# Latent attention of a two-layer block: keys and queries in tiles of 128 columns, rotary rows exchanged by Vector's shuffle, two query tiles moved behind the first score items

## The reference

```python
qa, ka, va, cq, ckv, kr, gates = jnp.split(h @ w_in, IN_SPLITS, axis=-1)
q  = heads(_rmsnorm(cq, g_q) @ w_uq, 8)      # 768 -> 8 heads x (64 plain + 32 rotary)
kv = heads(_rmsnorm(ckv, g_kv) @ w_ukv, 8)   # 256 -> 8 heads x (64 key + 64 value)
q_mla = _mla_q(qn, _axial_rope(qr, ang_r, ang_c))            # per head: 64 plain, 32 turned
k_mla = concat([k_ctx_mla, _mla_k(kn, _axial_rope(kr, ...))])  # one turned 32-row key for all heads
o_mla = softmax(q_mla @ k_mla.T * 96**-0.5) @ v_mla          # 8 heads, 512 x 768 scores
```

## Time and profile before

| what | value |
|---|---|
| median of 3 runs | 2316.14 us (2315.51 to 2317.17) |
| span of the profiled execution, first to last instruction | 2309.8 us |
| rotary key, latents and their norm, PE | 1612.8 to 1677.5 us |
| keys and values, PE | 1677.6 to 1705.1 us |
| queries, PE | 1705.1 to 1744.1 us |
| attention items 0 to 31 | 1744.1 to 1834.3 us |
| PE busy over the span | 2248.2 us (97%) |

### The profile page before, as it was taken

The page is one execution under the profiler, slowest core; times in us unless marked ns, Lnnn a source line. Parts: engine busy times, 40 slices in busy tenths (PEclk is TensorE's granted clock), DMA queues, the critical chain, the costliest instruction groups (busy, mean ns, idle before and its releaser), DMA issues.

```text
span 2309.8 us, 35228 instructions
## 1 busy us (share of the span) xinstructions
PE 2248.2 (97%) x12694; PEld 1935.9 (84%) x12694; DVE 1309.3 (57%) x2094; ACT 966.7 (42%) x1500; POOL 1300.6 (56%) x1448
## 2 busy tenths in 40 slices
PE   7999999999999999999999999999999999999997
PEld 6768787678888889999999979877866887999997
DVE  3424632498878778464454563243137556876666
ACT  4454544544233454332332343355435535444443
POOL 3434465099978766564654533322446064977775
PEclk9999999999999999999999999999999999999999
DMA  4222232255655542221222212222230031323232
GB/s 162 87 82 74 73 119 93 110 175 198 198 192 193 192 135 74 73 73 58 79 65 72 75 55 91 79 80 76 78 96 28 1 110 65 99 94 110 92 110 74
DMA packets 68241, 230.54 MB, mean 100 GB/s; under 512 B 7296, under 2 KB 12672, under 8 KB 67968
## 3 DMA queue, kind: packets, MB, share of 16 engines
q1 hardware_dynamic: 51232, 177.92, 23.3%
q10 hardware_dynamic: 16864, 50.60, 6.6%
HBM read 225.61 MB, written 2.10 MB: 99 GB/s over the span
## 4 chain that ended last, share of the span: by engine, by line
PE 82%; DVE 8%; issue 4%; ACT 3%; POOL 2%; DMA 0%; DVEq 0%; POOLq 0%; ACTq 0%; SPq 0%
PE ps L2304 20%; PE ps L2810 11%; PE ps L2308 10%; PE ps L2869 7%; PE ps L2866 6%; PE ps L2865 6%; PE ps L3013 4%; PE ps L2360 3%; POOL WLO L443 1%; PE ps L2315 1%; PE ps L2955 1%; PE ps L2984 1%; PE ps L2998 1%; PE ps L3152 1%; PE ps L3135 1%
## 5 line engine op out<-in xcount | busy, mean ns | idle before, releaser
L443 POOL TENSOR_TENSOR WLO<-RAW,WHI 128x256 fp32r<-128x256 f32 x1004 | 868.7, 900 | 739.3 <-ACT WHI L542 738.7
L542 ACT ACTIVATE WHI<-RAW 128x1024 fp32r<-128x1024 f32 x251 | 263.2, 1057 | 290.5 <-DMA RAW<-in_stream_dram 287.1
L462 POOL TENSOR_TENSOR WLO<-RAW,WHI 128x256 fp32r<-128x256 f32 x240 | 235.6, 1002 | 197.3 <-DVE SRAW L1913 82.4
L2304 PE MATMUL ps<-HLO,WHI 128*128 128x512 f32 (+2 forms) x872 | 317.4, 380 | 0.0
L2304 PE MATMUL ps<-HHI,WHI 128*128 128x512 f32 (+2 forms) x872 | 309.9, 371 | 0.0
L2308 PE MATMUL ps<-HHI,WLO 128*128 128x512 f32 (+2 forms) x872 | 198.4, 371 | 0.3 <-POOL WLO L443 0.3
L2304 PEld LDWEIGHTS ps<-HLO,WHI 128*128 128x128 f32 (+1 forms) x872 | 159.4, 188 | 33.5 <-issue 4.0
L2304 PEld LDWEIGHTS ps<-HHI,WHI 128*128 128x128 f32 (+1 forms) x872 | 159.3, 188 | 31.9 <-issue 3.4
L2308 PEld LDWEIGHTS ps<-HHI,WLO 128*128 128x128 f32 (+1 forms) x872 | 153.8, 188 | 29.2 <-POOL WLO L443 0.5
L2810 PE MATMUL ps<-GLO,WHI 128*128 128x384 f32 (+1 forms) x480 | 143.7, 353 | 1.3 <-POOL WLO L443 1.2
L2810 PE MATMUL ps<-GHI,WHI 128*128 128x384 f32 (+1 forms) x480 | 143.5, 353 | 0.0
(11 more groups left out here) (507 smaller groups left out, 5364.3 us busy)
## 6 DMA issues: line engine op xcount, KB each, us to landing
RAW<-in_stream_dram SPq DMA_DIRECT2D x331, 512.0 KB, 3.3
ADA<-in_ada_dram ACTq DMA_DIRECT2D x72, 512.0 KB, 4.4
BM<-in_bias_dram ACTq DMA_DIRECT2D x8, 448.0 KB, 3.7
DECAY<-in_decay_dram ACTq DMA_DIRECT2D x4, 512.0 KB, 4.2
C<-in_ctx_dram ACTq DMA_DIRECT2D x2, 1024.0 KB, 5.5
out_dram<-X SPq DMA_DIRECT2D x16, 128.0 KB, 1.8
X<-in_x_dram SPq DMA_DIRECT2D x2, 512.0 KB, 5.7
X<-in_x_dram ACTq DMA_DIRECT2D x2, 512.0 KB, 6.6
```

Of the source, the lines that this page charges most:

```text
L443: op = nc.gpsimd.tensor_tensor(WLO[:, slot(u), k:k + 2], RAW[:, slot(u), k:k + 2], WHI[:, slot(u), k:k + 2].bitcast(F32), ALU.subtract)
L462: op = nc.gpsimd.tensor_tensor(WLO[:, j, k:k + 2], RAW[:, j, k:k + 2], WHI[:, j, k:k + 2].bitcast(F32), ALU.subtract)
L542: nc.scalar.activation(WHI[:, j], RAW[:, j], ACT.Copy).then_inc(unit_hi, 1)
L2304: nc.tensor.matmul(out, high[k], x[:, k, tok], start=(k == 0 and n == 0), stop=False)
```

## The change

The weight columns of `w_ukv` and `w_uq` are laid out anew. The first `ukv` unit now holds the keys of all heads, two heads to a tile of 128 columns; the second holds all values. The `uq` units are six instead of eight: two tiles with the rotary rows of four heads each (32 rows a head, no padding), four tiles with the plain rows of two heads each. The permutation matrices are gone: DVE exchanges the rotary rows with `stream_shuffle` (i to i^8 in each group of 32 partitions). On PE the order becomes keys 0, keys 1, values 0 and 1, keys 2, values 2 and 3, keys 3, values 4 and 5, then four query tiles, score items 0 and 1, the last two query tiles, score item 2. ACT issues the eight key-spreading DMAs in one row after the keys, copies the last query tiles between exponentials of items 1 and 2, and rounds the weight units `o`+1 and `o`+2 inside the attention (after items 10 and 12) instead of beside the queries. `MP`, `MPT` and `KHI` change places. The constants shrink from seven 128x128 matrices to five.

```diff
-("ukv", 2), ("uq", 8), ("o", 8),
+("ukv", 2), ("uq", 6), ("o", 8),
+ROTATED = [i ^ 8 for i in range(32)]
-UKV_BANKS = (3, 2, 0, 1, 0, 1, 2, 3)
-UQ_BANKS = (3, 0, 1, 2)
+UKV_BANKS = (3, 2, 0, 1)
+MV_BANKS = (6, 7, 4, 5, 0, 1)
...
+        def roped_at(h):
+            return s("mq_rope"), 7 * (h // 4) + 3 + h % 4 + 1
...
-                sp.dma_start(const[:], t["const"][:, 0:7 * P]...
+                sp.dma_start(const[:], t["const"][:, 0:CONSTS * P]...
...
# POOL: lows(UNIT["na_q"], UNIT["o"] + 1) before the heads are split; split_head now waits
             pool.wait_ge(*attend_at("s", 3))
             pool.wait_ge(s("kr_spread"), 128)
+            pool.wait_ge(*roped_at(7))
...
# ACT, attend
+                    if n == 1:
+                        query_copy(2)
+                        query_copy(3)
+                    if n in (10, 12):
+                        convert(UNIT["o"] + n // 2 - 4)
...
# ACT, after the norm of cq
-            for h in range(8):
-                act.wait_ge(s("mk_ready"), h + 1)
-                nc.scalar.activation(MK[0:64, h], psf[0:64, at:at + N2], ACT.Copy).then_inc(s("mk"), 1)
+            for q in range(4):
+                if q < 3:
+                    act.wait_ge(s("mk_ready"), q + 1)
+                else:
+                    wait_unit(UNIT["ukv"])
+                for p in range(2):
+                    nc.scalar.activation(MK[0:64, 2 * q + p], psf[64 * p:64 * p + 64, at:at + N2], ACT.Copy).then_inc(s("mk"), 1)
+                if q == 1:
+                    convert(UNIT["ukv"] + AHEAD)
+                    act.dma_start(COSQ...); act.dma_start(SINQ...)
             convert(UNIT["ukv"] + AHEAD + 1)
-            act.wait_ge(s("kr_rope"), 3)
-            for h in range(8):
-                convert(UNIT["uq"] + AHEAD + h)
-                wait_unit(UNIT["uq"] + h)
-                nc.scalar.activation(q[0:QK_MLA, h % 4], ps[0:QK_MLA, UQ_BANKS[h % 4]], ACT.Copy).then_inc(s("mq_raw"), 1)
-                if h < 4:
-                    for i in (2 * h, 2 * h + 1):
-                        act.dma_start(MK[64:QK_MLA, i], KR2[64:QK_MLA]).then_inc(s("kr_spread"), 16)
+            act.wait_ge(s("kr_rope"), 4)
+            for i in range(8):
+                act.dma_start(MK[64:QK_MLA, i], KR2[64:QK_MLA]).then_inc(s("kr_spread"), 16)
+            convert(UNIT["uq"] + 3)
+            convert(UNIT["uq"] + 4)
+            def query_copy(a):
+                wait_unit(UNIT["uq"] + 2 + a)
+                bank = (4, 5, 7, 6)[a]
+                for p in range(2):
+                    nc.scalar.activation(query(2 * a + p)[0:64], ps[64 * p:64 * p + 64, bank], ACT.Copy).then_inc(s("mq_raw"), 1)
+            convert(UNIT["uq"] + 5)
+            query_copy(0)
+            convert(UNIT["o"])
+            query_copy(1)
...
# DVE
-                    if n == 1:
-                        query_rope(7)
+            def query_rope(i):
+                x, turned, n = ps[:, 6 + i], RQ[:, i], 7 * i
+                wait_unit(UNIT["uq"] + i)
+                V.stream_shuffle(turned, x, ROTATED)
+                V.tensor_tensor(x, x, COSQ[:], ALU.mult)
+                V.tensor_tensor(turned, turned, SINQ[:], ALU.mult)
+                for j in range(4):
+                    r = slice(32 * j, 32 * j + 32)
+                    V.tensor_tensor(query(4 * i + j)[64:QK_MLA], x[r], turned[r], ALU.add)
+            query_rope(0)
+            query_rope(1)
...
# PE, attend
+                    if n == 1:
+                        pe.wait_ge(*roped_at(7))
+                        query_tile(4, 7)
+                        query_tile(5, 6)
...
+                        if k == 0:
+                            pe.wait_ge(s("mq_raw"), 4)
# PE, before it
-            nc.tensor.matmul(ps[0:QK_MLA, 6], const[0:QK_MLA, SWAPM, 0:QK_MLA], KR2[0:QK_MLA, 0:S], ...)
+            def latent_keys(q):
+                pe.wait_ge(*norm_at("cq", *(("rs", 1), ("lo", 2), ("lo", 4), ("lo", 6))[q]))
+                mm = unit(UNIT["ukv"], 0, [(ps[:, 2 * j], x_tok), (ps[:, 2 * j + 1, 0:M], ctx_tok)], kt=2, k0=2 * q, ...)
+            def latent_values(b):
+                pe.wait_ge(s("mk"), 2 + 2 * (b // 2))
+                ... 6 matmuls of 512 columns into ps[:, MV_BANKS[b]]
+            latent_keys(0)
+            latent_keys(1)
+            wait_weights(UNIT["ukv"] + 1)
+            latent_values(0)
+            latent_values(1)
+            latent_keys(2)
+            latent_values(2)
+            latent_values(3)
+            latent_keys(3)
+            latent_values(4)
+            latent_values(5)
+            def query_tile(i, bank):
+                unit(UNIT["uq"] + i, 0, [(ps[:, bank], x_tok)], kt=6, hi=CQHI, lo=CQLO)
+            for i in range(4):
+                pe.wait_ge(s("mv"), i + 1)
+                query_tile(i, (6, 7, 4, 5)[i])
...
-                if n == 1:
-                    turn_query(7)
```

More of the change, by code:

```diff
@@ L267, in build, with query @@
         (MQBL,), _ = region(c_at, ("MQBL", [P, 4, S], F32R))
+        def query(h):
+            return MQA[:, h] if h < 4 else MQB[:, h - 4]
         def query_low(h):
@@ L3107, in turn_query @@
-            def turn_query(h):
-                pe.wait_ge(s("mq_raw"), h + 1)
-                if h >= 4:
-                    pe.wait_ge(s("mq_rope"), 3 * (h - 4) + 3)
-                nc.tensor.matmul(ps[0:QK_MLA, 4 + h % 4], const[0:QK_MLA, SWAPM, 0:QK_MLA], (MQA if h < 4 else MQB)[0:QK_MLA, h % 4],
-                                 start=True, stop=True).then_inc(s("mq_swap"), 1)
-            for h in range(8):
-                pe.wait_ge(*((s("mk"), 6), (s("mv"), 4), (s("mv"), 5), (s("mv"), 6))[h] if h < 4 else (s("mq_raw"), h - 3))
-                unit(UNIT["uq"] + h, 0, [(ps[0:QK_MLA, UQ_BANKS[h % 4]], x_tok)], kt=6, hi=CQHI, lo=CQLO, cols=(0, QK_MLA))
-                if h == 1:
-                    pe.wait_ge(s("mk"), 8)
-                if h:
-                    turn_query(h - 1)
+            def latent_keys(q):
+                pe.wait_ge(*norm_at("cq", *(("rs", 1), ("lo", 2), ("lo", 4), ("lo", 6))[q]))
+                j = UKV_BANKS[q]
+                mm = unit(UNIT["ukv"], 0, [(ps[:, 2 * j], x_tok), (ps[:, 2 * j + 1, 0:M], ctx_tok)], kt=2, hi=CVHI, lo=CVLO,
+                          k0=2 * q, last=(q == 3))
+                if q < 3:
+                    mm.then_inc(s("mk_ready"), 1)
@@ new lines, in latent_values @@
+            def latent_values(b):
+                pe.wait_ge(s("mk"), 2 + 2 * (b // 2))
+                j = slot(UNIT["ukv"] + 1)
+                for k in range(2):
+                    wh, wl = WHI[:, j, k:8:2, :], WLO[:, j, k:8:2, :]
+                    for n, (x, w) in enumerate(((CVHI, wh), (CVLO, wh), (CVHI, wl))):
+                        mm = nc.tensor.matmul(ps[:, MV_BANKS[b]], x[:, k, b * P:(b + 1) * P], w, start=(k == 0 and n == 0),
+                                              stop=(k == 1 and n == 2))
+                mm.then_inc(*((s("mv_ready"), 1) if b < 5 else (units_done, 1)))
@@ L3326, in layout @@
     w = g["w_ukv_2"][0]
-    for n in range(8):
-        units(UNIT["ukv"] + n // 4, w, P * n, n=1, k0=2 * (n % 4))
-    units(UNIT["uq"], g["w_uq_2"][0], cols=QK_MLA)
+    for part in range(2):
+        heads = w.reshape(2 * P, 8, 2, 64)[:, :, part].reshape(2 * P, 512)
+        for n in range(4):
+            units(UNIT["ukv"] + part, heads, P * n, n=1, k0=2 * n)
+    w = g["w_uq_2"][0].reshape(6 * P, 8, QK_MLA)
+    units(UNIT["uq"], w[:, :, 64:].reshape(6 * P, 256))
+    units(UNIT["uq"] + 2, w[:, :, :64].reshape(6 * P, 512))
     units(UNIT["o"], g["w_o_na_2"][0])
```

131 lines of the change are left out of this document (55 added, 76 removed).

## The result

The changed kernel takes **2289.46 us** in the median (2288.79 to 2290.53), beside 2316.65 for the kernel before (2315.51 to 2318.37) measured with it: a ratio of 0.9886, 95% interval 0.9872 to 0.9899. The forecast was 2291.8, with a range from 2289.5.

What follows compares the result with a forecast made beforehand. PE bounds the kernel, busy 2248.2 of 2309.8 us. Gains 0.86 + 6.0 + 18.5 = 25.4, less 1.0 and 0.2, plus 0.1, make 24.3 us; 2316.1 - 24.3 = 2291.8 us, range 2289.5 to 2295.5.

Steps and rivals of the forecast that it cites:

- rotary key: Ahead of the keys: its exchange on PE goes, DVE's shuffle does it unseen; gain 0.86 us.
- keys and values: Four key products instead of eight, six value tiles instead of two blocks, last ending at 1698.2; gain 6.0 us.
- queries to scores 4: Query tiles, items 0 and 1 and two moved tiles, up to scores 4 at 1729.6; gain 18.5 us.
- the rival of dearer columns: Keys and queries: matmul time goes by output columns, so only 10 us would go, 2306 us; chance 0.02.
- late weights: Rival before item 0: query weights or copies come late, PE waits 0 to 3.5 us, 2293.5 us; chance 0.10.
- its slack: Rotations on DVE: the second ends at 1712.7, needed only before the fifth query tile at 1717.3; no cost.
- the roundings: Attention, after items 10 and 12: two roundings of `o` on ACT delay copies and exponentials; cost 1.0 us, bounds 0 to 2.1.
- POOL beside DVE's scaling: Attention: POOL's remainders of the `o` units slow DVE's scaling beside them; cost 0.2 us, bounds 0 to 1.
- the rival that I had at 0.13: Keys and values: the hole lowers PE's clock, a loss of 1.7 to 3.4 us, time 2293.5 to 2295.2; chance 0.13.
- The hole itself: PE between keys 1 and values 0, waiting for ACT's key copies: 3.6 us, 1682.25 to 1685.85.
- The marks that the prediction set: Values end near 1698.2, scores 0 near 1714.8, scores 4 near 1729.6; one new 3.6 us hole, clock 1.00, no exchange matmuls.
- I carry the difference over: Whole run: the median 2316.14 lies 6.3 us above the profiled span of 2309.8, and the forecast keeps that difference.

Runs made afterwards that it cites:

- the one hole filled: Kernel before, with eight spare matmuls on constants in the 2.19 us hole ahead of item 1's transposes; 2313.40 us, ratio 0.9988.
- the tiles ahead of item 0: Changed kernel, with query tiles 4 and 5 ahead of item 0 instead of behind items 0 and 1; 2292.39 us, ratio 0.9894.
- the slow rotation: Changed kernel, with each rotation's shuffle done seven times instead of once; 2299.56 us, ratio 0.9918.
- the kernel with keys first: Changed kernel, with the four key tiles run first and the six value tiles behind them; 2285.63 us, ratio 0.9872.

## Why the prediction was right, and where it was wrong

In the profiled executions, term by term, with offsets read between the two traces:

| term | forecast | measured |
|---|---|---|
| rotary key | 0.86 | 0.87 (offset 1.26 to 0.39) |
| keys and values, last tile ended 1705.07, now 1701.59 | 6.0 | 3.9 |
| queries to scores 4, 1754.98 to 1732.64 | 18.5 | 18.9 |
| attention, scores 4 to the output projection, 79.09 to 80.09 us | -1.2 | -1.0 |
| start and unchanged code (-1.25 ahead of the change, +0.5 behind) | 0.1 | -0.75 |
| sum | 24.3 | 21.9 |

Of the 1.25 us ahead of the change, 1.15 arise between 484 and 495 us: there PE's first wait is shorter than in the kernel before (1.01 us beside 1.69) and its second longer (2.24 beside 0.42). The code there is not changed, and both forms occur in traces of the kernel before (1.08 and 2.24 with the one hole filled) and of the changed one (1.67 and 0.41 with the tiles ahead of item 0), so this is the execution and not the change.

**Right.** The rotary key, and the query tiles with the two moved ones: the largest term is 0.4 us off. A tile takes 2.72 + 1.36 us with 128 columns, beside 2.76 + 1.38 with 96, so the rival of dearer columns falls, and with it that of late weights: PE waits for none of the six. The shuffle's 0.75 us was as forecast, and its slack nearly; the slow rotation showed where the slack ends. In the attention the roundings cost 0.78 of the 1.0 I had put down. The rest, 0.2 us, is what I had put down for POOL beside DVE's scaling, but that it is POOL wasn't tried.

**Wrong, first: the keys and values.** The failing step is the choice of a clock at 1.00 behind the hole, and the rival that I had at 0.13 is what happens: the loss is 1.84 and 1.76 us in two profiles and 3.0 and 3.1 in two others, inside the 1.7 to 3.4 that I had worked out from the earlier trace rows. I had read the 2.85 us hole of the earlier trace rows, through which the clock stood, as evidence that a 3.6 us hole would probably pass. The trace of one execution does not say that: the clock also falls behind the 2.19 us hole of the earlier trace rows in one of the four profiles that have it. (Nor was the work before the fall at the end 0.7 us in 7: from the end of the spins, 2297.66, to 2303 it is 5.3.) By the rule of the Trainium skill that the prediction cited ("TensorE: Matmul & The Clock Gate", section "Why this matters for your kernels"), no long idle gaps between bursts, the term would have been 6.0 - 1.7 = 4.3, beside 3.9 measured; the traces agree with the rule for the holes of 3.45 and 5.10 us, behind which the clock fell each time. The remaining 0.3 of the 2.1 us that were missing is not traced to a cause. The hole itself was right (3.45 for 3.6). The marks that the prediction set are met less these things: scores 4 begin at 1732.64 instead of 1729.6, and the 3.0 us between are the clock's 1.84 and the 1.25 by which this execution was late before the change begins.

**Wrong, second: "I carry the difference over".** I took the 6.3 us between the median of the runs, 2316.14, and the span of the profile as fixed. Only 1.8 of it lies around the span. The other 4.5 was time that the profile did not show, and in the runs of the result it is gone: the changed kernel's profiled execution (2289.77) stands at the median (2289.46). On the second chip 1.5 us of it are left. About half of that time, 2.3 us (0.7 to 4.9), was the clock behind the hole at item 1, so it belongs to the change; for the rest that is not shown; I had priced the hole at its 2.19 us of waiting and not at what it does to the matmuls behind it.

The two errors nearly cancel: 24.3 - 21.9 = 2.4 us too much, 4.5 too little, and 0.2 to 0.3 for the spread of the changed kernel's own runs. That is why 2291.8 came out 2.3 over the time, and not because each step was good to 0.1%: it was luck. That the time touches the range is luck too: the low end's own terms, 2291.8 less 1.2 for the attention, 0.2 at the start and 0.6 for the spread, give 2289.8 and not 2289.5, and the measured 2289.46 lies under that.

What the change left behind is the order of keys and values. With the four key tiles first and the two roundings moved off items 10 and 12 the kernel takes 2284.71 us.

## What to carry to other kernels

When work is taken off an engine, lay out anew what stands between the pieces that are left: the removed key products had been covering ACT's copies, and their place became a hole that cost half as much again as its own length, in some executions nearly twice it. Before a sum is made on a profile, compare that execution's own time with the median of the runs: if it is quicker, ask which holes of the trace could cost more in the other executions, and treat the difference as part of what the change may move. When a wait must stay, put useful work of later stages into it first; spare matmuls do it too, if their length is measured, not guessed.

## What the runs showed of the hardware

The granted clock fell to 0.50 for 3.4 us in some executions and 6.8 in others behind the same hole at the keys; the price was 1.8 or 3.0 to 3.1 us. The low stretch did not always begin when PE resumed: in the changed kernel's first trace it did, in other traces it began while PE still stood idle, 0.97 us (tiles ahead of item 0) and 2.6 us (in front of the fifth query tile of the slow rotation: granted 1.00 up to 1726.5 and 0.50 from 1726.8, PE idle to 1729.37) before the next matmul.

A hole's length alone did not settle it. The 3.45 us hole had a fall in all four profiles that contain it, the 5.10 us hole in its one. The 2.19 us hole at item 1 had one in one profile of four, the second hole at 493 us, where it was 2.1 to 2.25 us long, in three of five. The first hole at 487 us, where it was 1.67 to 1.85 us long, had one in one of seven, and the 1.00 us hole at 263 us in one of fourteen. What decides in the shorter ones is open. This stretch, of the kernel with keys first, is the one behind 1.85 us at 487:

```profile
486.00:488.00 2.00, 0.59 (x2) 0.53 (x3) 1.30 (x2) 1.48 (x3) 2.00 (x4) 0.89 0.66 223
488.00:490.00 2.00, 2.00 (x7) 1.52 (x6) 2.00 (x3) 0.70 (x1) 2.00 (x2) 0.50 0.11 45
```

DVE's shuffle of 128x512 in f32 took 0.75 us from PSUM, near the 0.69 of a copy, with 0.01 us for its mask, and 0.73 when repeated; so the four groups of 32 partitions do not go one by one, for which 2.8 us had been the bound.
